# Norms behind the expert stages in two parts, context rows handed out earlier, and modulation tiles one by one in the first projection of a two-layer diffusion backbone on one core

## The reference

```
shift1, scale1, gate1, shift2, scale2, gate2 = split(silu(cond) @ w_mod[l] + b_mod[l])
h  = rms_norm(x, g1) * (1 + scale1) + shift1
qkv = h @ w_in[l]               # head groups A (6 heads, 2-D window + bias), B (4, differential), C (6 query / 2 key, normed)
x  = x + gate1 * (concat(oa, ob, oc) @ w_out[l])
h2 = rms_norm(x, g2) * (1 + scale2) + shift2
q  = h2 @ wq                    # 8 heads x 2 halves; top 16 of 128 keys on each half, top 16 of the 256 sums
x  = x + gate2 * sum_k softmax_k * gelu(u[e_k] . h2) * v[e_k]     # 8 x 16 = 128 experts per token, each a row of u and of v
```

## Time and profile before

| what | us |
|---|---|
| median of 3 runs | 4343.43 (4335.09 to 4356.98) |
| the profiled execution | 4348.79 |
| its span in the trace | 4346.8 |

### The profile page before, as it was taken

How to read it: one execution, slowest core, us unless ns; L and a number is a source line. 1 busy time by engine, 2 the same in 40 slices (tenths; PEclk the granted TensorE clock), 3 DMA queues, 4 the chain that set the end, 5 groups by cost and what they waited for, 6 DMA issues and landing times.

```text
span 4346.8 us, 47495 instructions
## 1 busy us (share of the span) xinstructions
PE 2888.6 (66%) x16560; PEld 1298.9 (30%) x16560; DVE 2806.7 (65%) x5854; ACT 1454.9 (33%) x4676; POOL 1292.9 (30%) x1306
## 2 busy tenths in 40 slices
PE   7897688775666666655556978886555555555554
PEld 4456565331221122321111566543111111111111
DVE  2166887697646756665675789669764775775444
ACT  2113675332223322222223468533222222222222
POOL 1002222123333333333343222212333333333332
PEclk9898889987777778778777989997778778777777
DMA  7536997569999999999997678666999999999996
GB/s 280 204 133 259 349 378 254 206 254 404 403 407 404 403 408 407 409 412 420 418 414 310 251 253 289 224 227 249 413 420 418 412 414 418 413 416 415 416 416 283
DMA packets 229151, 1508.71 MB, mean 347 GB/s; under 512 B 25392, under 2 KB 27440, under 8 KB 63920
## 3 DMA queue, kind: packets, MB, share of 16 engines
q0 software_dynamic: 185504, 1353.53, 77.7%
q1 hardware_dynamic: 43408, 152.14, 9.5%
HBM read 1501.38 MB, written 4.19 MB: 346 GB/s over the span
## 4 chain that ended last, share of the span: by engine, by line
DMA 41%; PE 25%; DVE 20%; issue 6%; ACT 5%; POOL 2%; SPq 0%; DVEq 0%; ACTq 0%; POOLq 0%
DMA work<-expert_dram,work 38%; PE psum L848 10%; DVE work L1694 5%; PE psum L876 4%; DVE work L1736 4%; PE psum L695 3%; DVE work L1744 3%; PE psum L786 2%; POOL work L1954 2%; DMA ring<-w_mod_dram 2%; PE psum L699 2%; ACT work L1207 1%; PE psum L763 1%; DVE stat L1484 1%; ACT work L1198 1%
## 5 line engine op out<-in xcount | busy, mean ns | idle before, releaser
L848 PE MATMUL psum<-work 64*64 64x512 f32 x8192 | 1422.0, 825 | 1121.8 <-ACT work L1207 1087.9
L1694 DVE SCALAR_TENSOR_TENSOR work<-work,psum 128x1024 f32<-128x1024 f32 x1024 | 1247.3, 1220 | 1001.9 <-DMA work<-expert_dram,work 996.9
L1954 POOL DMA_INDIRECT work<-expert_dram,work x1024 | 983.1, 960 | 1722.9 <-PE psum L848 1586.8
L848 PEld LDWEIGHTS psum<-work 64*64 64x64 f32 x8192 | 329.6, 168 | 2157.7 <-ACT work L1207 1841.9
L1198 ACT ACTIVATE work<-work 128x2 f32<-128x2 f32 x512 | 104.1, 203 | 1926.6 <-DVE work L1694 1910.0
L1936 POOL DMA_INDIRECT work<-expert_dram,work x256 | 279.5, 1092 | 1207.6 <-DVE work L1736 888.3
L1744 DVE SCALAR_TENSOR_TENSOR work<-work 128x1024 f32<-128x1024 f32 x256 | 311.3, 1217 | 92.3 <-DMA work<-expert_dram,work 91.8
L1207 ACT ACTIVATE work<-const,work 128x128 f32<-128x128 f32 x1024 | 347.3, 386 | 0.0
L1736 DVE SCALAR_TENSOR_TENSOR work<-work 128x1024 f32<-128x1024 f32 x254 | 325.2, 1280 | 19.7 <-ACT work L1223 19.3
L800 PE MATMUL psum<-work,ring 128*128 128x512 f32 x512 | 234.9, 614 | 28.5 <-ACT work L1070 28.5
L1201 ACT ACTIVATE work<-work 128x1 f32<-128x1 f32 x1024 | 245.7, 287 | 16.8
(11 more groups left out here) (197 smaller groups left out, 2864.9 us busy)
## 6 DMA issues: line engine op xcount, KB each, us to landing
ring<-w_mod_dram SPq DMA_DIRECT2D x96, 512.0 KB
ring<-w_in_dram SPq DMA_DIRECT2D x80, 512.0 KB
ring<-w_query_dram SPq DMA_DIRECT2D x64, 512.0 KB
work<-expert_dram,work POOLq DMA_INDIRECT x1280, 7.6
ring<-w_out_dram SPq DMA_DIRECT2D x32, 512.0 KB
work<-rpb_dram POOLq DMA_DIRECT2D x2, 2688.0 KB, 12.1
xT<-xT_dram SPq DMA_DIRECT2D x1, 2560.0 KB, 11.8
work<-tables_dram POOLq DMA_DIRECT2D x2, 1024.0 KB, 5.4
```

The source lines that it names most:

```text
L848: last = pe.matmul(out[to:to + HP, cols_], diag[tok, n % NDIAG, tok], rows[(SLOTS * t + s) % NBUF][tok, D + 512 * half:D + 512 * half + 51 ...
L1694: dve.scalar_tensor_tensor(u, u, 1.0, pair[0], ALU.mult, ALU.mult, accum_out=act_in[:, s:s + 1]).then_inc(dot_done, 1)
L1954: pool.indirect_dma_start(rows[m % NBUF], None, a[f"expert{l}"], bass.IndirectOffsetOnAxis(expert[:, t % 2, s:s + 1], 0)).then_inc(row_in[ ...
```

## The change

Four things are changed.

1. `FRONT_SEQ` takes the place of `FRONT_P`. The 32 modulation tiles ("m") no longer come in four runs of 8: they alternate singly with steps of the context front ("f") in windows 0 to 5. Their numbers per window are 10, 4, 5, 5, 4, 4; the context steps per window stay as before, but in window 5 seven of its eight stand behind the last chunk. The copies and turns of chunks 2 to 5 follow, in windows 1, 3, 4, 6 and 2, 4, 5, 7, and the banks of these chunks are 5, 4, 3, 5.
2. The norms behind an expert stage (`norm(2)` and the last) are done in two parts (`norm_parts`). For tokens 0 to 383 the squares stand on ACT at slots 20, 24 to 48 of the last tile, the sums on PE at 22, 26 to 50, the variance on DVE at slot 56, the root on ACT at 58, the reciprocal on DVE at 62, the multiplies on DVE at 64, 66 to 78, and scale and shift on ACT at 68, 70 to 82. Only tokens 384 to 511 are left for behind the last slot. The output is stored in two parts.
3. `ROW_CALLS` of layer 0: the projection gets 17 slots (2 in each of windows 13 to 16, 3 in each of 17 to 19) for 11, the pairs 68 for 76, the out-projection 18 for 14, the norm before the queries 2 for none, the queries 24 for 28. Within the pairs the 12 A pairs have 20 for 22, the others 48 for 54. Of the two in the norm one stands on DVE ahead of the wait for the sums, one between variance and reciprocal.
4. In layer 1 POOL issues the first five context gathers ahead of the loads of tables, caches and bias, as soon as the last row of the experts has been used, and not behind them and the last residual.

```
+FRONT_SEQ = [("fm", "fm", "fm", "mfmfmfmfmfmfmf"), ("fm", "", "", "mfmfmf"), ("fm", "fm", "fm", "mfmf"),
+             ("fm", "fm", "fm", "mfmf"), ("f", "fm", "f", "mfmfmf"), ("m", "m", "fm", "mfffffff"), ("f", "", "", "fff")]
+CHUNK_COPY = {chunk_place(c) + 1: c for c in range(2, 6)}
+CHUNK_TURN = {chunk_place(c) + 2: c for c in range(2, 6)}
-ROW_CALLS = [dict(P=[0] * (NWIN - 3) + [3, 4, 4], A=shares(76, NPAIR), O=shares(14, KC), Q=shares(28, HC)),
-             dict(P=shares(28, NWIN), A=shares(60, NPAIR), O=shares(12, KC), Q=shares(29, HC))]
+ROW_CALLS = [dict(P=[0] + [0] * 13 + [2] * 4 + [3] * 3, A=shares(68, NPAIR), O=[3, 2, 2, 2, 2, 2, 2, 3] + [2],
+                  Q=shares(24, HC)),
+             dict(P=[0] + shares(28, NWIN), A=shares(60, NPAIR), O=shares(12, KC) + [0], Q=shares(29, HC))]
+AHEAD = (LT - 1) * P
+AHEAD_SUM, AHEAD_VAR, AHEAD_MULT = 20, 56, 64
+def norm_parts(ni):
+    return ((0, AHEAD), (AHEAD, NLAT)) if ni and ni % 2 == 0 else ((0, NLAT),)
...
+            for part, (lo, hi) in enumerate(norm_parts(2 * L)):
+                sp.wait_ge(y_ready, part + 1)
+                sp.dma_start(a["out_yT"][:, :, lo:hi], h[:, :, lo:hi]).then_inc(y_stored, 16)
...   PE, in a slot of the experts
+                        if t == LT - 1 and s >= AHEAD_SUM + 2 and s % 4 == 2 and s < AHEAD_SUM + 2 + 4 * KC:
+                            if s == AHEAD_SUM + 2:
+                                pe.wait_ge(y_added, LT * l + LT - 1)
+                            square_sum(2 * l + 2, (s - AHEAD_SUM - 2) // 4)
...   PE, in the first projection
-                            for m, j in project_mods(l, i):
-                                mod_tile(m, j)
-                            go(front, FRONT_P[i][PARTS.index(k)])
+                            for x in FRONT_SEQ[i][PARTS.index(k)]:
+                                if x == "f":
+                                    go(front, 1)
+                                else:
+                                    mod_tile(0, next(mods))
...   ACT, in the slots of the last tile
+            def ahead(ni, s):
+                c = (s - AHEAD_SUM) // 4
+                if s % 4 == 0 and 0 <= c < KC:
+                    if c == 0:
+                        act.wait_ge(y_added, LT * (ni // 2) - 1)
+                    square(ni, c)
+                if s == AHEAD_VAR + 2:
+                    root(ni // 2, -1, var_ahead)
+                c = (s - AHEAD_MULT - 4) // 2
+                if ni < 2 * L and 0 <= c < KC:
+                    affine(ni, c)
...   DVE, in the slots of the last tile
+            def ahead(ni):
+                dve.wait_ge(sum_step, norm_count(ni) + KC)
+                dve.tensor_scalar(var_ahead, psum[:, 2, 0:AHEAD], 1.0 / D, EPS, ALU.mult, ALU.add).then_inc(var_ready, 1)
+                yield
+                dve.wait_ge(sd_ready, roots(ni // 2, -1))
+                link(dve.reciprocal(rs_ahead, var_ahead))
+                yield
+                for c in range(KC):
+                    scaled(ni, c, 0, rs_ahead)
+                    yield
...   POOL, at the start of layer 1
+                    pool.wait_ge(row_used, SLOTS * LT * l)
+                    calls += ROW_CALLS[l]["P"][0]
+                    ctx_gather(l, calls)
                     pool.wait_ge(y_added, LT * l)
```

More of the change, by code:

```diff
@@ L559, in build @@
         PROJ = NWIN + HC
-        ROOTS_L = 2 + 4
+        ROOTS_L = 3 + 4
         def roots(l, i):
@@ L675, in post @@
                     pe.wait_ge(post_fin, POSTS * l + p - 1)
+                if l == 0 and p == 1:
+                    pe.wait_ge(mod_read, 4)
                 if what == "norm":
@@ L685, in project @@
             def project(l, front):
+                mods = iter(range(16, NMOD))
                 for i in range(NWIN):
@@ L1046, in mod_copy, with square, affine, norm @@
                 last.then_inc(mod_row, 1)
-            def square(ni, c):
+            def square(ni, c, part=0):
+                lo, hi = norm_parts(ni)[part]
+                dst = sq_ahead if hi == AHEAD else sq
                 if c >= 2:
-                    act.wait_ge(sum_step, KC * ni + c - 1)
-                act.activation(sq[:, c % 2, :], xT[:, c, 0:NLAT], ACT.Square).then_inc(sq_ready, 1)
-            def norm(ni):
+                    act.wait_ge(sum_step, norm_count(ni, part) + c - 1)
+                act.activation(dst[:, c % 2, 0:hi - lo], xT[:, c, lo:hi], ACT.Square).then_inc(sq_ready, 1)
+            def affine(ni, c, part=0):
+                l, m = ni // 2, 3 * KC * (ni % 2)
+                lo, hi = norm_parts(ni)[part]
+                act.wait_ge(y_mult, norm_count(ni, part) + c + 1)
+                act.activation(h[:, c, lo:hi], h[:, c, lo:hi], ACT.Identity, bias=modT[:, l, m + c, 0:1],
+                               scale=modT[:, l, m + KC + c, 0:1]).then_inc(h_done, 1)
+            def norm(ni, slots):
                 if ni == 0:
@@ L1066, in norm, with root @@
                 if ni < 2 * L:
-                    l, m = ni // 2, 3 * KC * (ni % 2)
                     for c in range(KC):
-                        act.wait_ge(y_mult, KC * ni + c + 1)
-                        act.activation(h[:, c, :], h[:, c, :], ACT.Identity, bias=modT[:, l, m + c, 0:1],
-                                       scale=modT[:, l, m + KC + c, 0:1]).then_inc(h_done, 1)
-            def root(l, i):
+                        affine(ni, c, part)
+                    go(slots, norm_calls(ni))
+            def root(l, i, x):
                 act.wait_ge(var_ready, roots(l, i))
-                act.activation(var, var, ACT.Sqrt).then_inc(sd_ready, 1)
+                act.activation(x, x, ACT.Sqrt).then_inc(sd_ready, 1)
             def project(l, front, slots):
@@ L1358, in _ @@
                 slots = ctx_slots(l)
-                norm(2 * l)
+                norm(2 * l, slots)
                 project(l, front, slots)
@@ L1362, in _ @@
                 out_projection(l, slots)
-                norm(2 * l + 1)
+                norm(2 * l + 1, slots)
                 queries(l, slots)
@@ L1366, in _ @@
                 experts(l, front)
-            norm(2 * L)
+            norm(2 * L, None)
         @block.vector
@@ L1431, in norm @@
                 else:
-                    root(l, 5 if half else 0, psum[:, 2, :], D)
-                if ni == 2 * L:
-                    for c in range(KC):
-                        last = dve.scalar_tensor_tensor(h[:, c, :], xT[:, c, 0:NLAT], col("fgain", c), rs,
-                                                        ALU.mult, ALU.mult)
-                    last.then_inc(y_ready, 1)
-                    return
+                    root(l, 5 if half else 0, psum[:, 2, lo:hi], D, slots, calls // 2, var[:, lo:hi], rs[:, lo:hi])
                 for c in range(KC):
-                    dve.tensor_tensor(h[:, c, :], xT[:, c, 0:NLAT], rs, ALU.mult).then_inc(y_mult, 1)
+                    scaled(ni, c, part, rs[:, lo:hi])
             def project(l, front, slots):
@@ L1683, in experts @@
                 places = front_places(l, DVE_LATER)
+                early_norm = ahead(2 * l + 2)
+                ahead_at = [AHEAD_VAR, AHEAD_VAR + 6] + [AHEAD_MULT + 2 * c for c in range(KC)]
                 def dots(t, n):
```

116 lines of the change are left out of this document (74 added, 42 removed).

## The result

The changed kernel takes 4309.62 us (median of 12 runs, 4302.01 to 4325.98) against 4338.91 (12 runs): ratio 0.9933, interval 0.992 to 0.9945, 29 us less. The forecast was 4265, with a range of 4240 to 4305: right in sign, and out of the range by 5 us, since it promised 74 to 78. The profiled execution took 4312.1 us, its span is 4310.0, 36.8 under that of before; the profiled execution of before took 10 us more than its median.

What follows compares the result with a forecast made beforehand. No engine was taken to hold the end alone; stages were priced singly. First projection -25.7, context rows -31, layer 1 entry -12.8, end -10.9, slot work +2 sum to -78.4: 4348.8 to 4270, by the median 4265, range 4240 to 4305.

Steps and rivals of the forecast that it cites:

- First projection: -26: Layer 0's first projection: spreading modulation tiles singly removes PE's waits for their loads; -25.7 us, ends -38 and -10.
- -48.1, +16: First projection: the four runs of 8 tiles last 48.1 us but hold 16 us of work; spreading removes the rest.
- -36.8: First projection: the gain in us if window 5 had no stall.
- Rival B: First projection gains only 10 us, as context steps on DVE and ACT pace the windows; total 4281, chance 0.22.
- +11.1 for window 5: First projection, window 5: PE stands still about 9 us ahead of step 33, plus 2.1 of slow restart.
- Context rows: Layer 0: moved row slots save 31 us: attention start -5, A pairs -8, other pairs -12, out-projection and norm 0, queries -6.
- The check by layer 1: Pairs: slots set the pace, since layer 1 with 60 slots and no modulation tiles takes 240 us against 319.
- Rival C: Layer 0: moved slots shorten neither pairs nor queries, PE and ACT carrying them; 26 us lost, total 4291, chance 0.13.
- Rival E: Projection and A-pair rows take a full round trip, 8.3 us a slot; total 4356, or 4438 with A pairs; chance 0.04.
- The norms: Norms behind expert stages in two parts: layer 1's entry -12.8 us, the end -10.9, work in slots +2.
- Rival D: Last expert tiles: norm work in the slots is exposed by late ring refills; +47 us, total 4312, chance 0.08.
- ACT's detour: Last expert tile: after a 2.87 us ACT detour the dot a ring later waited 1.25 as ever; evidence against exposed work.

Runs made afterwards that it cites:

- (1): Kernel before with only the modulation tiles spread singly; rows, norms and POOL's order as before: 4342.31 us, ratio 1.0005 to the kernel before.
- (2): Changed kernel with its modulation tiles back in four runs of 8 in windows 0 to 3: 4306.82 us, ratio 0.9935 to the kernel before.
- (3): Changed kernel with the first projection's 32 modulation tiles computed on on-chip constants, taking no ring block (wrong numbers): 4282.4 us, ratio 0.9872 to the kernel before.
- Experiments 4: Changed kernel with as many tiles per window, all behind the window's last chunk: 4307.96 us, ratio 0.9938 to the kernel before.
- 5: Changed kernel with 13, 6 and 5 modulation tiles in windows 0 to 2, the last 8 in windows 7 to 14: 4289.77 us, ratio 0.9893 to kernel before.
- experiment 12: Kernel with the tiles placed anew, layer 1's context rows 36 for 28 in projection, 50 for 60 in pairs, 14 for 12 in out-projection: 4310.37 us.
- experiment 9: Changed kernel with layer 1's 48 modulation tiles, in layer 0's pairs, computed on constants without ring blocks (wrong numbers): 4285.57 us, ratio 0.9873 to kernel before.
- experiment 11: Kernel with the tiles placed anew, 20 context rows for 17 in windows 13 to 19, 65 for 68 in pairs: 4291.73 us, ratio 0.9881 to kernel before.
- experiment 7: Changed kernel with the norms behind the expert stages in one part, as before: 4327.9 us, ratio 0.9971 to the kernel before.
- experiment 8: Changed kernel with POOL's first five context gathers of layer 1 back in their old place: 4315.09 us, ratio 0.9939 to the kernel before.

## Why the prediction was wrong

**The failed step** is "First projection: -26", in it the terms "-48.1, +16". The sum took the whole of the four runs as waits that spreading removes, since each tile's load would lie "beside a context step". It never asked when a load can be issued. The waits for tiles and context blocks come to 24.4 us (18.4 + 3.2 before); 18.1 of them sit behind the release of a window's block, in six places. The runs show it from three sides: the change alone gives 0 (1), its undoing loses nothing (2), taking the tiles out of the ring gives 32 us (3). The size of the terms would have fitted that last case: without the stall the forecast was -36.8, and experiment 3 has -32.1 against the kernel before, with 6.9 us more of stall. What was wrong is that spreading hides the loads. Experiments 4 and 5 show that the order can be chosen so that other blocks and work cover part of the load; the change's order, a tile right behind the window's last chunk with three blocks taken before it, asks for that block as soon as it is issued. Rival B's gain of 10 is nearer than -26, but its mechanism is not what held PE (3). The forecast's +11.1 for window 5 was right in kind and too large: the stall grew by 4.4 us, and the first work behind it took 1.7 more (L1047 1.97 for 1.09, L925 15.27 for 14.45).

**Context rows** (-31 forecast, about -10 measured). The step that failed is the price of a row in the pairs: I took 4.0 and 2.0 us, near the mean stage time per row and near the DMA time of one, and it is 2.2 and 0.6. The check by layer 1 (240 us with 60 rows and no tiles) mixed two differences; experiment 12 shows that rows hardly matter there, and experiment 9 that the tiles' bytes matter more. Rival C (rows shorten nothing) was nearer for the pairs; the queries went as forecast. The start of attention was 0 to +2.7 for -5. Rival E's delay appears only above 17 rows (experiment 11), and the price beyond them is 4.4 us a row, not 8.3.

**The norms** (-21.7 forecast, some -17 by the times of experiment 7) were near in each term: entry -13.7 for -12.8, tail -14.9 for -14.8, 4.8 us for the store and work in layer 1. The entry's figure depends on POOL's order: without the two parts the entry is 176.0 or 171.9, and so they are worth 13.5 or 9.4. Rival D is out: its 47 us are not there, and layer 0 shows none of it within its spread of 16. The row that said so was ACT's detour.

**The table load.** The Trainium skill's "ScalarE: Activation LUTs" (What ACT_TABLE_LOAD costs) would add 1.38 us of drain per switch. In the changed kernel's tail too the root follows its load at once, as in the earlier trace rows; no drain is seen:

```profile
4301.30 1.28 ACT L1135 ACT_TABLE_LOAD   x1
4302.59 0.31 ACT L1135 ACTIVATE work<-work 128x128 f32<-128x128 f32 x1
```

**POOL's order**: 0 forecast, none seen with the norm in two parts (experiment 8).

## What to carry to other kernels

A wait for a transfer is removed by issuing the transfer earlier or by putting other work ahead of its use: before spreading loads, follow each buffer of the ring from its release to the next issue, and look for a block that is held long, since it closes the ring for all behind it. Price work moved between stages by the difference of two stages with more and less of it, not by stage time divided by count or by a busy share, and expect a knee: here a row cost 0 up to the 17th and 4.4 us from the 18th to the 20th in one place, 1.3 and then 3.1 in another.

## What was not expected of the hardware

The time from the issue of a 512 KB load to PE's use of it was 3.4 to 3.8 us when the ring had nothing else under way (58.62 to 62.02, 141.13 to 144.97; three more loads were issued within 1.4 us behind each), against 1.3 us a block at full flow. Behind such a wait TensorE's granted clock was 0.50 (145 to 153), and with the loads gone PE's busy time fell by 12.8 us beside 19.5 of idle time (experiment 3). A stage of 512 gathers with the same instructions varied by 16 us between profiles, so a few us in it can't be read from two profiles. And the last store, in 1024 pieces each time, moved at 283 to 297 GB/s with pieces of 512 B and at 363 to 398 GB/s with pieces of 2 KB.
